# V rows of one stage moved from VectorE to ScalarE and Pool

## What is computed

```python
h = rmsnorm(x) * (1 + scale1) + shift1
p = h @ w_in                       # gated linear recurrence and attention read its columns
o_a = hgrn2_mixer(...)             # the scans, two directions
o_b = attention(...)
y = (sigmoid(gA) * (o_a @ w_oa) + sigmoid(gB) * (o_b @ w_ob)) @ w_out
x = x + gate1 * y
h2 = rmsnorm(x) * (1 + scale2) + shift2
# PEER: 8 heads x 16 experts for each token
act = gelu(einsum('nhkd,nd->nhk', take(w_u, idx), h2))
x = x + gate2 * einsum('nhk,nhkd->nd', g * act, take(w_v, idx))
```

## Time and profile before

| | |
|---|---|
| median of 3 runs | 2533.73 us (2533.69 to 2540.07) |
| the profiled execution | 2531.67 us, of which the span from first to last instruction is 2529.9 us |
| busy | PE 79%, DVE 69%, ACT 39%, POOL 37% of the span |
| mean granted TensorE clock | 0.923 of full speed |
| mean DMA rate | 318 GB/s |

### The profile page before, as it was taken

The page is one execution under the profiler, slowest core; times in us unless marked ns, Lnnn a source line. Parts: engine busy times, 40 slices in busy tenths (PEclk is TensorE's granted clock), DMA queues, the critical chain, the costliest instruction groups (busy, mean ns, idle before and its releaser), DMA issues. The chain is left out here.

```text
span 2529.9 us, 27355 instructions
## 1 busy us (share of the span) xinstructions
PE 2007.2 (79%) x6925; PEld 1115.7 (44%) x6925; DVE 1749.0 (69%) x3969; ACT 977.8 (39%) x2481; POOL 940.1 (37%) x774
## 2 busy tenths in 40 slices
PE   6978899946566679988698876877878787787876
PEld 2677846835555544476454222322223222232222
DVE  2732278888776768667787777777777777777764
ACT  1402145244444344412333434444444444344443
POOL 0020012222221222202233554656645665456654
PEclk9998999968787789989899999999989999899999
DMA  8844678853332369959798999999999999999997
GB/s 323 289 150 157 224 294 332 306 187 131 116 101 100 117 234 345 340 213 402 270 374 318 421 422 390 422 422 422 421 403 422 422 422 421 403 414 422 422 422 323
DMA packets 113299, 805.53 MB, mean 318 GB/s; under 512 B 12596, under 2 KB 14006, under 8 KB 17046
## 3 DMA queue, kind: packets, MB, share of 16 engines
q0 software_dynamic: 93760, 680.96, 67.3%
q1 hardware_dynamic: 17704, 118.17, 12.7%
q10 hardware_dynamic: 1712, 4.98, 0.5%
HBM read 800.79 MB, written 3.28 MB: 318 GB/s over the span
## 5 line engine op out<-in xcount | busy, mean ns | idle before, releaser
L1213 POOL DMA_INDIRECT RG<-in_uv,idxs x264 | 357.9, 1356 | 561.6 <-DVE pl L1440 326.9
L957 ACT ACTIVATE agel<-apre 128x1 f32<-128x1 f32 x640 | 129.2, 202 | 944.8 <-DVE apre L1412 940.9
L600 PE MATMUL pl<-RG,BP 128*128 128x512 f32 x576 | 296.6, 641 | 106.8 <-ACT BP L973 103.5
L600 PE MATMUL pl<-RING,BP 128*128 128x512 f32 x576 | 282.0, 621 | 60.7 <-ACT BP L973 57.7
L1412 DVE CUSTOM_DVE_ANT_0 R<-RG,AB 128x1024 f32<-128x1024 f32 x201 | 246.6, 1230 | 103.5 <-DMA RG<-in_uv,idxs 84.3
L1213 POOL DMA_INDIRECT RING<-in_uv,idxs x168 | 248.1, 1477 | 159.3 <-issue 71.0
L1412 DVE CUSTOM_DVE_ANT_0 R<-RING,AB 128x1024 f32<-128x1024 f32 x168 | 206.0, 1226 | 95.1 <-DMA RING<-in_uv,idxs 77.4
L625 PE MATMUL pa<-HL,RING 128*128 128x512 f32 (+2 forms) x800 | 243.3, 461 | 1.1 <-DMA RING<-in_pq_slabs 1.0
L600 PEld LDWEIGHTS pl<-RG,BP 128*128 128x128 f32 x576 | 100.4, 193 | 295.8 <-ACT BP L973 219.2
L973 ACT ACTIVATE BP<-CT,wexp 128x128 f32<-128x128 f32 x480 | 192.7, 401 | 47.8 <-PE pl L600 9.9
L600 PEld LDWEIGHTS pl<-RING,BP 128*128 128x128 f32 x576 | 104.4, 194 | 232.5 <-ACT BP L973 135.0
(11 more groups left out here) (288 smaller groups left out, 3285.6 us busy)
## 6 DMA issues: line engine op xcount, KB each, us to landing
RING<-in_in_slabs SPq DMA_DIRECT2D x42, 1024.0 KB
RING<-in_pq_slabs SPq DMA_DIRECT2D x24, 1152.0 KB
RING<-in_ada_slabs SPq DMA_DIRECT2D x16, 1024.0 KB
RING<-in_out_slabs SPq DMA_DIRECT2D x12, 1024.0 KB
RG<-in_col_slabs POOLq DMA_DIRECT2D x8, 1024.0 KB, 7.0
RING<-in_o_slabs SPq DMA_DIRECT2D x8, 1024.0 KB
RG<-in_uv,idxs POOLq DMA_INDIRECT x297, 6.1
RING<-in_uv,idxs POOLq DMA_INDIRECT x168
```

What stands on the lines that cost most here:

```text
L600: last = nc.tensor.matmul(acc[:, c * 512:(c + 1) * 512], DG[:, k % 2, :], bufs[k % len(bufs)][:, D + c * 512:D + (c + 1) * 512], start=Fal ...
L957: A(agel[:, par, k:k + 1], apre[:, par, k:k + 1], ACT.Gelu).then_inc(gel_done, 1)
L1213: nc.gpsimd.indirect_dma_start(out=bufs[b], out_offset=None, in_=uv, in_offset=bass.IndirectOffsetOnAxis(ap=idxs[:, par, k:k + 1], axis=0) ...
```

## The change

For the 40 slots 46 to 85, those placed in the stage "merged", the V row leaves DVE. ACT multiplies the V half of the gather's buffer in place with the slot's weight (an activation Copy over 128x1024), and POOL adds it to an accumulator of its own, `PACC`, in SBUF. `PACC` is the scratch `SCR[1]`, so the dots of tile 0 now all write `SCR[0]`, and each waits for the dot before. POOL clears `PACC` once, ahead of slot 0. It does its add right in front of the gather that reuses the buffer, four slots later. After the gates and the last slots of tile 0, DVE adds `PACC` to `PL` once (`folded`), and ACT's load of the norm's row into `SCR[1]` waits for that.

```diff
+PV_FROM, PV_TO = STAGES[0][1], STAGES[0][1] + STAGES[1][1]
+        PACC = SCR[1]
     # ACT, w_slot
                 if not diagonal and isinstance(n, int) and n < TSLOT:
-                    act.wait_ge(v_done, n - 1 + V0)
+                    act.wait_ge(v_done, n - (7 if PV_FROM <= n < PV_TO + 8 else 1) + V0)
                 A(wexp[...], agel[...], ACT.Copy, scale=gws[...]).then_inc(w_done, 1)
+                if not diagonal and isinstance(n, int) and PV_FROM <= n < PV_TO:
+                    act.wait_ge(w_done, n + 1)
+                    A(GA[n % NGA][:, D:2 * D], GA[n % NGA][:, D:2 * D], ACT.Copy,
+                      scale=wexp[:, par, k:k + 1]).then_inc(vs_done, 1)
     # ACT, norm_rows
+                if t == 0:
+                    act.wait_ge(folded, 1)
     # POOL
+            def pool_v_row(n):
+                pool.wait_ge(vs_done, n - PV_FROM + 1)
+                pool.wait_ge(v_done, n + V0)
+                if n == PV_FROM:
+                    pool.wait_ge(pacc_clear, 1)
+                nc.gpsimd.tensor_tensor(PACC, PACC, GA[n % NGA][:, D:2 * D], ALU.add).then_inc(v_done, 1)
             def gather(n, k, par, bufs, sems, slot_wait):
+                if isinstance(n, int) and PV_FROM <= n - NGA < PV_TO and n < TSLOT:
+                    pool_v_row(n - NGA)
...
             pool.sem_inc(v_done, V0)
+            pool.memset(PACC, 0.0).then_inc(pacc_clear, 1)
     # DVE, dot_of
-                dve.wait_ge(u_done, n - 1 + U0)
-                V.tensor_tensor_reduce(out=SCR[k % 2], ...
+                alone = isinstance(n, int) and n < TSLOT
+                dve.wait_ge(u_done, n - (0 if alone else 1) + U0)
+                V.tensor_tensor_reduce(out=SCR[0 if alone else k % 2], ...
     # DVE, static_slot
-                if (t == 0 and n) or (t and k % 2):
+                if (t == 0 and n and not PV_FROM <= n - 1 < PV_TO) or (t and k % 2):
                     v_row(n - 1)
     # DVE, after the gates
             mix(1)
             beside.rest()
+            dve.wait_ge(v_done, TSLOT - 1 + V0)
+            step(V.tensor_tensor(PL[:, :], PL[:, :], PACC, ALU.add), folded)
             beside.open(1)
```

More of the change, by code:

```diff
@@ L441, in build @@
                                                                 sem("w_done"), sem("dg_done"), sem("v_done"))
-        vp_done, yp_out = sem("vp_done"), sem("yp_out")
+        vp_done, yp_out, pacc_clear, folded = sem("vp_done"), sem("yp_out"), sem("pacc_clear"), sem("folded")
+        vs_done = sem("vs_done")
         acc_closed, acc_read, fss_ready, frt_ready, y_ready = (sem("acc_closed"), sem("acc_read"), sem("fss_ready"),
@@ L1409, in dot_of @@
             def dot_of(buf, n, k, par, hc):
-                dve.wait_ge(u_done, n - 1 + U0)
-                V.tensor_tensor_reduce(out=SCR[k % 2], in0=buf[:, 0:D], in1=hc, scale=1.0, scalar=0.0,
+                alone = isinstance(n, int) and n < TSLOT
+                dve.wait_ge(u_done, n - (0 if alone else 1) + U0)
+                V.tensor_tensor_reduce(out=SCR[0 if alone else k % 2], in0=buf[:, 0:D], in1=hc, scale=1.0, scalar=0.0,
                                        op0=ALU.mult, op1=ALU.add, accum_out=apre[:, par, k:k + 1]).then_inc(u_done, 1)
```

## The result

The changed kernel takes 2561.89 us (median of 4 executions, 2557.01 to 2562.7) against 2533.71 us for the kernel before on the same chip: ratio 1.0103, interval 1.0086 to 1.012. The forecast was 2528.9 us with a range up to 2556; the kernel is 28 us slower than before, outside the range. The profiled execution has a span of 2555.1 us, 25.2 us more than before.

The account below looks back on a forecast made before the run. DVE was taken to lead 0.88 of 528 to 912 us, with later stretches following; -42.2 (V rows) + 33.4 (adds) + 4 (POOL's updates) = -4.8 us, so 2528.9 us by the median, range 2508 to 2556.

Parts of the forecast that it names:

- The change alters neither, but both simply follow what lies ahead: 912 to 1140 us (PE) and from 1380 us (DMA): whatever 528 to 912 us gains or loses, the run does.
- the stalls of DVE: Scans: POOL's adds hold DVE operations with two SBUF inputs, 38 us, x 0.88 = 33.4 us more.
- POOL's updates: Scans: POOL's own updates move and meet DVE's forward update and dot, 4 us more (0 to 9).
- 29 single adds: Scans: 29 of 40 adds stand alone; 23 meet a held operation, 32.5 us together; six meet none.
- That 1.3: Slot 61: the add runs from 662.2 to 664.7 and catches step L1655 at 663.29, costing DVE 1.3 us.
- In the pairs: 11 adds in pairs of slots: the second dot goes ahead of the add; 0.5 us each, 5.5.
- the lock costs more than the V rows: Rival for the scans: adds catch the dots in pairs, all levels held; +17 us, about 2550; chance 0.21.
- break-even: That rival's threshold: a mean stall of 1.2 us per add, less 0.1 for the updates.
- V rows removed: Scans: 40 V rows at 1.20 us leave DVE, x 0.88 = 42.2 us less (34 to 48).
- The share of DVE's time that reaches the end: 528 to 912 us: DVE leads for 0.88 of the stretch, so 0.88 of what it is spared or charged counts.
- The shorter estimate: POOL's add at 2.25 us, half the skill page's 4497 ns; sum 9 us lower, 2520; as a rival, chance 0.04.
- The fold: Behind DVE's last product of the gates: 1.28 us inside a wait for PE, costing nothing, or 1.5 us.

Follow-up runs that it names:

- the padded runs with and without adds: Changed kernel plus 78 semaphore increments at DVE's program start: whole adds, 2538.24 us; POOL adding only 8 of 1024 columns, 2493.15 us.
- the padded kernel: Changed kernel with 78 semaphore increments, which nothing waits for, at the start of DVE's program: 2538.24 us, ratio 1.0018 against the kernel before.
- the kernel with more products: V rows through PE by a diagonal of the weight, no POOL add or fold, DVE padded by 81: 2515.18 us, ratio 0.9924 against the kernel before.

## Why the prediction was wrong, point by point

**The step that failed** is in the first part: "The change alters neither, but both simply follow what lies ahead", of 912 to 1140 us and of all from 1380 us on. It cost 20.9 of the 25.2 us by which the profiled execution grew. The edit took 78 instructions out of DVE's program, and in tiles 3 and 4 DVE then stood 4.6 to 5.0 us at four jumps back, and twice 3.0 us behind. Padding takes this away and shifting the kernel before brings it about, so the cause, the position of the loops in DVE's program, is shown. That the stall is the fetch of instructions fits queue 14 (22 packets more) and was not measured more directly.

The Trainium skill ("Runtime: NRT & Kernel Launch", section "Instruction fetch mechanics") states a rule that I did not weigh: instructions come in blocks of 256, two at a time, and a jump back to a block that is no longer there waits for a fetch. The traces agree as far as the count of places above goes: the bodies that by it span two blocks show no stall, those that span three do. The page gives no figure for it; here it was 4.6 to 5.5 us for each jump, and some 10 us for each tile. Not all of the idle time reaches the end: in tile 4 of the changed kernel the four stretches add up to 15.3 us, and the tile is 10.5 us longer; in tile 3 two add up to 9.6, and it is 10.4 us longer. Why the stretches behind cost next to nothing, no run tested.

**The mis-sized term** is the stalls of DVE: 38 us forecast for the adds and some 4.5 for POOL's updates, some 51 us measured as growth of its other work (50 us as the difference of the padded runs with and without adds). On the way to the end it was 46.4 us, against 33.4 + 4 forecast. The mechanism was right. Laid beside the undisturbed length of each operation, the 40 adds hold DVE for 49.0 us. Of the 29 single adds 24 meet an operation and cost 37.8 us (23 and 32.5 us forecast): many catch the L1676 step at its start, 2.2 us for slot 61, where I had 1.3. That 1.3 was read from the old timeline, in which the V row still stands between the dot (658.86) and the step (663.29), 4.43 us apart. With the V row gone the step starts 1.2 us sooner, 3.24 us behind the dot of 667.55, and that is where the add starts too. In the pairs I took 0.5 us each, on the ground that the second dot goes ahead of the add and what follows reads PSUM or one input. That held for five of them (48, 64, 68, 72, 80); the other six met something later on: the routing step L1395 for slots 50 and 82 (2.1 us each), the copy L1378, which has one input, for 58 (2.3) and 74 (1.3), a dot for 77 (2.1), the L1676 step for 84 (1.3). That is 11.2 us, not 5.5. POOL's own updates were a small term: they held DVE for 5.1 us before and for 6.6 after, 1.5 us more, where some 4.5 were forecast. The rival "the lock costs more than the V rows" is what happened in the scans: its +17 of upper bounds became +7, that is -39.3 for the V rows and +46.4 for the adds. Its break-even was a mean of 1.2 us for each add less 0.1; the adds held 1.23 us each.

**What held.** V rows removed: 42.2 us forecast, 39.3 measured. The share of DVE's time that reaches the end: 0.88 forecast; without the adds 49.9 us of DVE's time gave 46.4 us, 0.93. The add, 2.54 us forecast, took 2.53 and 2.35 in the mean. The 2.53 fits by luck, since 2.35 is what an undisturbed add takes. The shorter estimate, worked out from the Trainium skill ("GPSIMD Engine Reference", section "Elementwise — side-by-side cycle accounting"), was 2.25, and the undisturbed add is nearer to that. The scaling took 1.15 us and hid behind ACT's waits. PE waits for POOL 17.1 us against 17.0, as said. The fold took 1.23 us behind the last product of the gates, where PE was waited for anyway:

```profile
1088.90 1.23 DVE L1825 TENSOR_TENSOR pl<-pl,R 128x1024 f32<-128x1024 f32 x1
1094.39 0.42 DVE L1740 TENSOR_TENSOR HG<-pa,G1L 128x256 f32<-128x256 f32 x1 [4.25 <-PE pa L628]
```

Had the tail stayed as it was, the result would have been that of the padded kernel, 2538.24 us: inside the range and within 0.3% of no change, though with the stalls 9 us too low in the sum.

## What to carry to other kernels

Work that goes from DVE to POOL costs DVE time wherever a DVE operation of the kind that is held falls into POOL's instruction. In these traces those are operations with two SBUF inputs, but also copies and scalings from SBUF to SBUF of more than one number per partition (L1378, L1607, L1646, L1678). Those that read PSUM, the maxima, the reductions and the scaling of one number (L1666) ran on unheld. Price it as POOL's duration times the chance to meet one, cut long POOL instructions into a few pieces, or give the work to an engine that doesn't hold DVE, as PE here. And every edit that changes the number of instructions ahead of a loop moves the loop: before a result is believed, look for idle time without a releaser behind the jumps back and at the packets of the instruction queue, and repeat the edit with the old number of instructions. Here that part was 20.9 us, and the scans, which the change was about, lost 7.0.

## What was unexpected of the hardware

- The position of a loop in an engine's program is worth 21 us of 2530 here, with no change in the work: 78 semaphore increments that nothing waits for made the changed kernel 23.7 us faster, and 178 made the kernel before 18.2 us slower (medians).
- A POOL instruction holds even a very small DVE operation to its end: one number per partition added to another took 2.36 us beside an add of 2.35 us. It works the other way too: the add that started 0.57 us into a dot took 2.86 us. The operation that is held loses the rest of POOL's instruction less some 0.15 us, and only one of the 40 adds held two operations.
- Four adds of 256 columns take 3.5 us together where one of 1024 takes 2.35 to 2.5, and the kernel with them is still 0.6% faster than the padded one.
- In the kernel with more products the mean granted clock in the scans rose from 0.77 to 0.88 of full speed, so more of the stretch ran at 2.4 and less at 1.2 GHz, while PE's busy time rose from 239 of 384 to 292 of 372 us.
